# Order of the exps and of the R, K and kk_a hats in the RWKV recurrence of a hybrid layer

## What is computed

```
def step(S, inp):
    r_t, w_t, k_t, v_t, a_t, b_t = inp
    sa = jnp.einsum('bhvk,bhk->bhv', S, a_t)
    S = S * w_t[:, :, None, :] + sa[..., :, None] * b_t[..., None, :] + v_t[..., :, None] * k_t[..., None, :]
    return S, jnp.einsum('bhvk,bhk->bhv', S, r_t)
...
decay = to_heads(jnp.exp(-jnp.exp(w)))
a = to_heads(jax.nn.sigmoid(lp['rw_a0'][d] + a_lo @ lp['rw_a2'][d]))
kd = kh * (1.0 + (a - 1.0) * k_a)
y, s_fin = wkv7_scan(rh, decay, kd, vh, -kk, kk * a, s0[d], reverse=(d == 1))
```

## Time and profile before

| | |
|---|---|
| median of 3 runs | 2461.0 us (2460.78 to 2463.07) |
| the profiled execution | 2462.29 us; its span 2460.6 us |
| mean granted TensorE clock in it | 0.969 |
| TensorE (PE) busy | 2263.6 us, 92% |
| VectorE (DVE) busy | 1551.8 us, 63% |
| ScalarE (ACT) busy | 1009.5 us, 41% |
| GpSimd (POOL) busy | 265.3 us, 11% |
| the local recurrence's units | 1310.4 to 1788.8 us of the span |

### The profile page before, as it was taken

The page is one execution under the profiler, slowest core; times in us unless marked ns, Lnnn a source line. Parts: engine busy times, 40 slices in busy tenths (PEclk is TensorE's granted clock), DMA queues, the critical chain, the costliest instruction groups (busy, mean ns, idle before and its releaser), DMA issues. The chain is left out here.

```text
span 2460.6 us, 66375 instructions
## 1 busy us (share of the span) xinstructions
PE 2263.6 (92%) x26630; PEld 1853.4 (75%) x26630; DVE 1551.8 (63%) x2611; ACT 1009.5 (41%) x1734; POOL 265.3 (11%) x335
## 2 busy tenths in 40 slices
PE   4999999999899999999947899999788799899998
PEld 2788878888688887888836777777657576688887
DVE  5756566666865456665635777777456676856754
ACT  5444234544532123445424555555333666411111
POOL 0000000000000000000031222222124663000000
PEclk7999999999999999999978999999978899999999
DMA  7344333333242333333330111110068523834542
GB/s 240 107 135 125 111 94 111 113 117 102 94 129 93 96 108 97 106 111 119 107 101 25 32 41 32 32 56 17 19 214 305 126 94 95 288 115 171 197 152 88
DMA packets 250306, 277.75 MB, mean 113 GB/s; under 512 B 30683, under 2 KB 174171, under 8 KB 247643
## 3 DMA queue, kind: packets, MB, share of 16 engines
q1 hardware_dynamic: 245306, 266.95, 33.9%
q10 hardware_dynamic: 4576, 8.40, 0.9%
q0 software_dynamic: 320, 0.98, 0.2%
HBM read 184.66 MB, written 91.62 MB: 112 GB/s over the span
## 5 line engine op out<-in xcount | busy, mean ns | idle before, releaser
L715 PE MATMUL proj_ps<-h_hi,w_hi 128*128 128x512 f32 x1656 | 649.5, 392 | 27.6 <-DVE h_lo L465 19.7
L716 PE MATMUL proj_ps<-h_lo,w_hi 128*128 128x512 f32 x1656 | 647.0, 391 | 0.0
L717 PE MATMUL proj_ps<-h_hi,w_lo 128*128 128x512 f32 x1656 | 646.4, 390 | 0.0
L318 ACT CAST w_hi<-w_raw 128x512 fp32r<-128x512 f32 x420 | 255.1, 621 | 694.0 <-PE proj_ps L717 353.2
L715 PEld LDWEIGHTS proj_ps<-h_hi,w_hi 128*128 128x128 f32 x1656 | 312.3, 189 | 98.2 <-issue 26.1
L717 PEld LDWEIGHTS proj_ps<-h_hi,w_lo 128*128 128x128 f32 x1656 | 312.2, 189 | 65.6
L716 PEld LDWEIGHTS proj_ps<-h_lo,w_hi 128*128 128x128 f32 x1656 | 312.4, 189 | 62.9
L482 DVE TENSOR_TENSOR w_lo<-w_raw,w_hi 128x512 fp32r<-128x512 f32 x420 | 283.2, 689 | 44.3 <-ACT w_hi L318 43.7
L498 DVE TENSOR_TENSOR z_slots<-proj_ps,x_rows 128x512 f32<-128x512 f32 x174 | 120.2, 691 | 169.9 <-PE proj_ps L717 167.9
L498 DVE TENSOR_TENSOR x_rows<-proj_ps,x_rows 128x512 f32<-128x512 f32 x116 | 80.1, 691 | 108.9 <-PE proj_ps L717 102.9
L1010 POOL MEMSET rpb_padded<- 60x127 f32 x1 | 0.2, 198 | 1261.3 <-POOLq L89 1261.3
(11 more groups left out here) (380 smaller groups left out, 4101.4 us busy)
## 6 DMA issues: line engine op xcount, KB each, us to landing
w_raw<-in_w_in SPq DMA_DIRECT2D x240, 256.0 KB, 3.0
scratch_gatesT<-z_slots SPq DMA_DIRECT2D x128, 256.0 KB, 2.7
late_rows<-scratch_gatesT SPq DMA_DIRECT2D x64, 512.0 KB, 4.4
scratch_zT<-z_slots SPq DMA_DIRECT2D x108, 256.0 KB, 2.4
ada<-in_ada_w SPq DMA_DIRECT2D x4, 2048.0 KB, 15.2
late_rows<-scratch_zT SPq DMA_DIRECT2D x4, 2048.0 KB, 12.7
late_rows<-scratch_branchT SPq DMA_DIRECT2D x16, 512.0 KB, 5.3
late_rows<-in_x SPq DMA_DIRECT2D x16, 512.0 KB, 4.9
```

The costliest lines, as they stand in the source:

```text
L318: A.copy(wh[:, i, :, :], raw[:, q, :, :]).then_inc(w_hi, 1)
L715: T.matmul(out, wh[:, i, k, :], hi[:, o, k, :], start=(first and k == 0), stop=False, skip_group_check=not first)
L716: T.matmul(out, wh[:, i, k, :], lo[:, o, k, :], start=False, stop=False, skip_group_check=not first)
L717: last = T.matmul(out, wl[:, i, k, :], hi[:, o, k, :], start=False, stop=(k == 3), skip_group_check=not first)
```

## The change

ScalarE's exps for the next unit move: while (n, 1) runs, from behind the At. copy to ahead of the X4 and Z4 copies; while (n, 0) runs, to just ahead of the At. copy. VectorE's hats are cut in two. `hats_early` makes R and K, and for a next unit of d = 1 also kk_a, and stands ahead of the mask of the fifth G, behind kd (and, for d = 1, behind the bonus rows). What is left of `hats` makes B and A, in that order, with kk and kk_a ahead for d = 0, and stands behind that mask as before. TensorE's first scores wait for "A", now the last of the hats, in place of "B". No operation is added or removed.

```
--- before.py
+++ after.py
@@ -920,7 +920,7 @@
         block_v = [f"mix{j}" for j in mixes] + ["ksq"] + newton + ["kk"]
         block_a = [f"scaled{j}" for j in mixes] + ["th", "kkr0", "kkr1", "rrk0", "rrk1"]
         prep_v = Turns(ctx, nc, "prep_vector", [f"mix{j}" for j in mixes] + ["ksq", "lw", "L", "Lx", "inc"] + newton
-                       + ["kd", "kds", "bt", "kk", "R", "kka", "A", "K", "B", "bonus"], U,
+                       + ["kd", "kds", "bt", "R", "K", "kk", "kka", "B", "A", "bonus"], U,
                        leaves_out=(("Lx", "inc", "kds", "bt", "bonus"), block_v))
         prep_a = Turns(ctx, nc, "prep_scalar", [f"scaled{j}" for j in mixes]
                        + ["th", "kkr0", "kkr1", "tw0", "tw1", "rrk0", "rrk1", "ta0", "ta1", "u0", "u1", "EI", "EN", "tot"], U,
@@ -1133,23 +1133,27 @@
                 prep_v.own(dve, (n, 1), V.tensor_tensor(kds[:], kd[:, 0], kd[:, 1], ALU.add), "kds")
                 prep_v.done(V.tensor_tensor(kds[:], kds[:], rrk[:], ALU.mult), 1, "bt")
 
+            def hats_early(n, d):
+                done = lambda ins, name: prep_v.done(ins, d, name)
+                prep_a.after(dve, (n, d), "tot")
+                if not (first_block(n) and d == 0):
+                    main_g.after(dve, (n, d), "R.", back=1)
+                done(V.tensor_tensor(chunks(AR[:, 1, :, :]), chunks(zf[:, 0:2, :]), padded(d, 1 - d), ALU.mult), "R")
+                prep_v.after(dve, (n, d), "kd")
+                done(V.tensor_tensor(Kh[:], kd[:, d], EN[:], ALU.mult), "K")
+                if d:
+                    done(V.scalar_tensor_tensor(kka[:], aa[:], 1.0, kk[:], ALU.add, ALU.mult), "kka")
+
             def hats(n, d):
                 done = lambda ins, name: prep_v.done(ins, d, name)
                 if d == 0:
                     prep_p.after(dve, (n, 0), "rnT")
                     done(V.tensor_tensor(kk[:], kkr[:], ps[:, 7, :].rearrange("p (m t) -> p m t", m=2), ALU.mult), "kk")
-                prep_a.after(dve, (n, d), "tot")
-                if not (first_block(n) and d == 0):
-                    main_g.after(dve, (n, d), "R.", back=1)
-                done(V.tensor_tensor(chunks(AR[:, 1, :, :]), chunks(zf[:, 0:2, :]), padded(d, 1 - d), ALU.mult), "R")
-                if d == 0:
                     prep_v.after(dve, (n, 0), "kk")
-                done(V.scalar_tensor_tensor(kka[:], aa[:], 1.0, kk[:], ALU.add, ALU.mult), "kka")
-                done(V.scalar_tensor_tensor(chunks(AR[:, 0, :, :]), chunks(kk[:]), -1.0, padded(d, d), ALU.mult, ALU.mult), "A")
-                prep_v.after(dve, (n, d), "kd")
-                done(V.tensor_tensor(Kh[:], kd[:, d], EN[:], ALU.mult), "K")
+                    done(V.scalar_tensor_tensor(kka[:], aa[:], 1.0, kk[:], ALU.add, ALU.mult), "kka")
                 prep_v.after(dve, (n, d), "kka")
                 done(V.scalar_tensor_tensor(Bh[:], kka[:], 0.5, EN[:], ALU.mult, ALU.mult), "B")
+                done(V.scalar_tensor_tensor(chunks(AR[:, 0, :, :]), chunks(kk[:]), -1.0, padded(d, d), ALU.mult, ALU.mult), "A")
 
             bits = lambda a: a.bitcast(mybir.dt.int32)
             strict_of = lambda d: flat(tri[:, d, :, :]).rearrange("p (o k) -> p o k", o=1).to_broadcast([P, 8, 2 * CH])
@@ -1180,6 +1184,7 @@
                 decay(0, 0)
                 norms(0)
                 rates(0, 0)
+                hats_early(0, 0)
                 hats(0, 0)
                 dve.wait_ge(masks.sem, N_MASKS)
                 for d in range(2):
@@ -1232,6 +1237,7 @@
                         rates(*nxt)
                         if d == 0:
                             bonus_rows(n)
+                        hats_early(*nxt)
                 if nxt:
                     hats(*nxt)
                 if d == 0:
@@ -1361,12 +1367,14 @@
                     own(A.copy(flat(Vt[:]), ps[:, 6, :]), "V.")
                 if nxt:
                     key_rates(*nxt)
+                    if d:
+                        exps(*nxt)
                 factor(X[:], "X4.", 4)
                 factor(Z[:], "Z4.", 0)
+                if nxt and d == 0:
+                    exps(*nxt)
                 main_p.after(act, (n, d), "A.")
                 own(A.copy(eights(WI[:, :, :, :, 0:CH]), ps[:, 6:8, 0:256].rearrange("p q (k t) -> p q k t", t=CH)), "At.")
-                if nxt:
-                    exps(*nxt)
                 main_p.after(act, (n, d), "MV.")
                 own(A.copy(eights(WI[:, :, :, :, CH:P]), ps[:, 4:6, 0:256].rearrange("p q (k t) -> p q k t", t=CH)), "MV.")
                 factor(Z[:], "Z5.", 0)
@@ -1427,7 +1435,7 @@
                 prep_p.done(last, 0, "rnT", *left_out)
 
             def first_scores(u, back):
-                prep_v.after(pe, u, "B", back)
+                prep_v.after(pe, u, "A", back)
                 go()
                 for g, m, q, c in tiles:
                     both = ps[half(c), 2 + q, :].rearrange("p (a k t) -> p a k t", a=2, t=CH)[:, :, g * 2 + m, :]
```

## The result

| | before | changed |
|---|---|---|
| median of 4 runs | 2462.03 us (2460.78 to 2466.05) | 2502.76 us (2495.96 to 2511.29) |
| ratio | | 1.0164 (95% interval 1.0130 to 1.0198) |
| profiled execution, its span | 2462.29, 2460.6 us | 2504.1, 2502.3 us |
| mean granted clock | 0.969 | 0.958 |
| even unit, from its first G product to that of the next unit | 25.26 us | 27.32 to 29.63 us |

The change makes the kernel 41 us slower, by the interval 32 to 49 us. The direction was forecast, the size was not: 22.4 us, 2475 to 2492.

What follows compares the result with a forecast made beforehand. TensorE's list sets the pace, with GY moving each unit: 8 even x 2.05 = 16.4, 8 odd x 0.74 = 5.9, first unit 0.8, prologue -0.7, sum +22.4 on 2461.0, forecast 2483.4 us, range 2475 to 2492.

Steps and rivals of the forecast that it cites:

- The chain and the even unit: Unit (n, 0) preparing (n, 1): mask 2.59 us late, 0.49 won at the first scores, GY 2.05 us late.
- the prologue: Before the first unit: R and K fill VectorE's 0.67 us idle time, first scores start 0.7 us earlier.
- First unit: First unit of the local recurrence: its fifth mask is 0.8 us late, taken as a loss of 0.8 us.
- The odd unit: Unit (n, 1) preparing (n+1, 0): mask 1.21 us late, 0.48 won at the first scores, GY 0.74 us late.
- the clock: TensorE ahead of Z5 in even units: new idle pieces of 1.2 us or so leave the full clock.
- a granted clock below 1.00: Sign in the changed kernel's local recurrence stage that the forecast would be wrong; the forecast took the full clock.
- the second rival: Clock falls in the even units, Z5 to end of W: 2.2 us more, 9 times, 20 us, 2503; chance 0.06.
- The late copy of the A hats: ScalarE, even unit: copy some 1.3 us late, costed at nothing under TensorE's pause before Z5; uncovered, up to 1.3 us.
- VectorE had no slack and nothing was won: Rival 1: VectorE has slack, units hang on the scores' wait; 8.3 us won in the units, 2452; chance 0.04.
- loss and gain did not cancel: Rival 4: loss at the mask and gain at the scores cancel, within 5 us of before; chance 0.02.
- The odd units did not lose nothing: Rival 3: odd units' 0.74 us hidden, or even units' loss hidden twice; 4 to 6 us less, 2478; chance 0.08.

Runs made afterwards that it cites:

- The filler: Changed kernel plus two matmuls of a constant into unread product columns, in TensorE's pause ahead of the fifth mask's wait: 2487.26 against 2465.70 us before, ratio 1.0084.

## Why the prediction was wrong

**The chain and the even unit: right.** Mask 2.59 us late, GY 2.05, with the 0.49 won at the scores taken off: at full clock the trace has 2.59 and 2.04, and the unit 27.32 us. In the prologue the first scores start 4.46 us behind the products of the transposed norms, where it was 4.97: 0.51 earlier, against 0.7. First unit and the stages around can't be told from the scatter of single traces: the first unit is 28.96 us in the trace of before, and 31.0 in that of the kernel with the exps moved in the odd units alone, which has no change there. Over all thirteen kernels the first unit starts at 1309.9 to 1313.6 us, and the span ends 694 to 703 us behind the start of the last one.

**The odd unit: mis-sized.** The step was "Moving two ahead of the mask ... makes the mask 2 x 0.605 = 1.21 us late", GY 0.74. Measured: the mask 1.63 late (19.37 against 17.74), GY 1.15, the unit 27.94, 1.12 over before. The missing 0.42 is R at 1.10 us beside GpSimd's copy. I took VectorE's operations to be 0.60 apart wherever they stand; R was moved into the time of a copy of GpSimd's, beside which no hat had stood in the loop. Moving the copy away took the 0.42 back: R took 0.69 us there, against 1.10 beside the copy.

**The step that failed: the clock.** It was "The new idle pieces, of 1.2 us or so, are nearer to the 0.9, so I take the full clock", although the prediction itself named a granted clock below 1.00 as a sign of being wrong. The stage's units 0 to 16 took 449.32 us before and 494.40 after, 45.1 more. By the units that kept their clock the waits make 7 x 2.06 + 8 x 1.12 = 23.4 in the loop, where the two sorts of unit grew by 22.9 + 16.7 = 39.6 in all (the even units 2 to 14, the odd ones 1 to 15): 16.2 us are lost clock. That is the second rival in kind, which had 20 us, 2503, and a chance of 0.06; but it had the loss in the even units alone, and the odd ones lose as much, 7.7 against 8.5. That the measured 2502.76 falls on its 2503 is luck. In the odd units the pause was longer than I had seen: I had priced its 1.21 us of delay in the sum and never asked what it made of TensorE's idle time, which is the 0.30 of before, the 1.21 and R's 0.42: 1.93 us in one piece. Without R's 0.42 it would have been 1.51, and at that no odd unit lost the clock (GpSimd's copy later). In the even units the step failed by itself: pieces of 1.05 and 1.36 us, about what I had named, cost clock in five of seven. The filler shows that the pause is the cause, R alone ahead of the mask that a shorter one is free. The sum, from these two traces: the forecast's 22.4, 16.2 for the clock in the loop, 3.0 for R, 2.6 more than forecast in the first unit and the last even one; the first unit starts 3.1 later where it was to start 0.7 earlier, and what lies behind the last unit's start is 6.4 shorter, both inside the scatter just named. That makes the 41.7 us between the two spans, to 0.1. The clock fell here behind 1.93 us of idle TensorE and less, though not at every wait; the waits that the prediction had held against the full clock were 3.87 and 3.88 us long.

**The late copy of the A hats: right.** In the changed kernel it is covered. "Without that cover it would be up to 1.3 us": the kernel with ScalarE's part alone has Z5 1.09 later and, with the scores' wait won back, the even unit 0.62 longer. My expectation of that kernel had it only as the rival, and that of R and K ahead of the mask in the odd units alone left it out.

**The other rivals.** VectorE had no slack and nothing was won, and loss and gain did not cancel. The odd units did not lose nothing: each lost at least 1.12 us.

## What to carry to other kernels

An engine's wait that one shortens is worth only what the next limit leaves of it, and what is put ahead of the operation on the chain costs in full: here 0.5 us could be won at the scores, and 1.6 to 2.6 were spent at the mask. Ask of each added delay whether TensorE stands idle for it in one piece, and price the clock with it: a pause of 1.9 us in one piece cost another 1.3 us or so in six of eight odd units, one of 1.5 us cost nothing in any; in the even units two pieces, 1.05 and 1.36 us with the transposes between them, brought it down as well, in five of seven here and in two of seven with GpSimd's copy later. Length is not all: with VectorE's part alone 2.94 us in one piece cost clock in two of seven. So take such a cost as a range, and look for it in the trace. Before moving an operation ahead, look whether one that the waiting engine does not read can be moved back: B ahead of K took 0.5% off the time, and nothing waited for the later K.

## What was not expected of the hardware

The clock falls in short stretches (0.50 from 1593.9 to 1597.3 us above) and comes back while TensorE goes on working: TensorE is busy all 3.40 us of that stretch, and 4.39 of the 4.92 behind it, at 1.00. In one kernel some units lose it and others of the same shape don't (even units from 27.32 to 29.63 us in one trace). The changed kernel's four runs span 15 us, and with the filler 5; whether that is the clock is not shown, since 19 runs of the kernel before, whose loop held the clock in its trace, span 16.

Which of VectorE and GpSimd is slowed seems to hang on who is first. R, begun 0.39 us into GpSimd's copy of 128 x 512, took 1.10 us in place of 0.69; kd, already running when that copy began, took its usual 0.68, and it was the copy that took 0.95 in place of 0.61. Before the change a mask of products stood where R now stands, and was not slowed (0.68 us). With GpSimd's copy later, B is the one that begins beside it in the odd units, 0.37 us into the copy, and takes 0.98 us; kk_a, already running, keeps its 0.69, and the copy takes 0.81. It costs nothing more there. That is read from timelines, and only the cost to R was tested.
